# A new order of head pairs and projection tiles, merged products in latent attention, and two reordered steps at stage boundaries

## The reference: what is computed

```python
s_w = jnp.einsum('bqkgd,bskd->bkgqs', q_n, k_n).astype(jnp.float32) * scale      # windowed
p_w, p_c, _ = _multi_softmax([s_w, s_c, sink_col])
s_n = jnp.einsum('bwhd,bwnhd->bhwn', q_r, k_nb).astype(jnp.float32) * scale + bias.astype(jnp.float32)
```

```python
q = (_rmsnorm(c_q, q_norm) @ w_uq).reshape(B, S, MLA_HEADS, MLA_NOPE_DIM + MLA_ROPE_DIM)
q_rope = _apply_rope(q[..., MLA_NOPE_DIM:], cos[:, None], sin[:, None])
kv = (_rmsnorm(c_kv, kv_norm) @ w_ukv).reshape(B, S, MLA_HEADS, MLA_NOPE_DIM + MLA_V_DIM)
```

## Time and profile before

| | us |
|---|---|
| median of 3 runs | 2383.7 (2381.66 to 2384.02) |
| profiled execution, its own time | 2387.36 |
| its span, first to last instruction | 2386.1 |
| PE busy | 2279.2 (96%) |
| DVE busy | 1497.5 (63%) |
| ACT busy | 959.8 (40%) |
| mean granted TensorE clock | 0.979 |

### The profile page before, as it was taken

The page is one execution under the profiler, slowest core; times in us unless marked ns, Lnnn a source line. Parts: engine busy times, 40 slices in busy tenths (PEclk is TensorE's granted clock), DMA queues, the critical chain, the costliest instruction groups (busy, mean ns, idle before and its releaser), DMA issues. The chain is left out here.

```text
span 2386.1 us, 37057 instructions
## 1 busy us (share of the span) xinstructions
PE 2279.2 (96%) x14376; PEld 1925.4 (81%) x14376; DVE 1497.5 (63%) x2306; ACT 959.8 (40%) x1540; POOL 368.1 (15%) x365
## 2 busy tenths in 40 slices
PE   6999999998999999999999999879999999998998
PEld 4888887765678888878888876669998998798998
DVE  4666766545775666676664346466667766676874
ACT  4222223454542222242222245444446434555763
POOL 1000001000000000000000010039995476000000
PEclk9999999999999999999999999989999999999999
DMA  7554444111134444434443241114544332234544
GB/s 281 185 188 175 172 167 168 71 36 53 54 128 163 168 178 161 167 136 159 174 177 121 97 141 54 70 58 156 191 170 151 114 108 72 88 135 157 187 168 149
DMA packets 52615, 331.05 MB, mean 139 GB/s; under 512 B 6544, under 2 KB 7824, under 8 KB 21648
## 3 DMA queue, kind: packets, MB, share of 16 engines
q1 hardware_dynamic: 49040, 319.15, 37.0%
q0 software_dynamic: 3456, 10.25, 1.4%
HBM read 325.56 MB, written 3.80 MB: 138 GB/s over the span
## 5 line engine op out<-in xcount | busy, mean ns | idle before, releaser
L1181 PE MATMUL bank<-u_hi,whi 128*128 128x512 f32 (+1 forms) x2512 | 865.2, 344 | 29.2 <-DVE u_lo L1135 13.6
L1182 PE MATMUL bank<-u_lo,whi 128*128 128x512 f32 (+1 forms) x2512 | 849.8, 338 | 0.0
L1183 PE MATMUL bank<-u_hi,wlo 128*128 128x512 f32 (+1 forms) x2512 | 849.2, 338 | 0.0
L568 DVE TENSOR_TENSOR wlo<-raw,whi 128x2048 fp32r<-128x2048 f32 (+2 forms) x207 | 434.9, 2101 | 314.9 <-ACT whi L566 314.8
L1181 PEld LDWEIGHTS bank<-u_hi,whi 128*128 128x128 f32 x2512 | 477.3, 190 | 104.7 <-issue 30.3
L1183 PEld LDWEIGHTS bank<-u_hi,wlo 128*128 128x128 f32 x2512 | 477.4, 190 | 52.1
L1182 PEld LDWEIGHTS bank<-u_lo,whi 128*128 128x128 f32 x2512 | 477.5, 190 | 49.5 <-issue 0.2
L566 ACT ACTIVATE whi<-raw 128x2048 fp32r<-128x2048 f32 (+2 forms) x207 | 353.1, 1706 | 338.5 <-PE bank L1183 234.1
L1243 ACT ACTIVATE sil<-bank 128x512 f32<-128x512 f32 (+1 forms) x88 | 48.0, 545 | 543.6 <-PE bank L1183 543.5
L1181 PE MATMUL bank<-hidden_hi,whi 128*128 128x512 f32 x528 | 205.4, 389 | 0.0
L1182 PE MATMUL bank<-hidden_lo,whi 128*128 128x512 f32 x528 | 205.4, 389 | 0.0
(11 more groups left out here) (426 smaller groups left out, 2938.7 us busy)
## 6 DMA issues: line engine op xcount, KB each, us to landing
raw<-in_stream SPq DMA_DIRECT2D x231, 1024.0 KB, 4.8
raw<-in_stream SPq DMA_DIRECT2D x80, 704.0 KB, 4.0
first_ada<-in_stream SPq DMA_DIRECT2D x8, 1024.0 KB, 16.5
raw<-in_stream SPq DMA_DIRECT2D x8, 768.0 KB, 4.4
skew<-rpb_rows POOLq DMA_DIRECT2D x8, 336.0 KB, 6.1
nbr_bias<-skew POOLq DMA_DIRECT2D x24, 112.0 KB, 3.5
h<-in_tokens SPq DMA_DIRECT2D x1, 2048.0 KB, 11.6
uq_ukv<-in_small POOLq DMA_DIRECT2D x1, 1536.0 KB, 8.1
```

What stands on the lines that cost most here:

```text
L568: v.tensor_tensor(self.lo[to][:, 0:n], raw[:, 0:n], self.hi[to][:, 0:n].bitcast(F32), ALU.subtract).then_inc(self.s_lo, 1)
L1181: pe.q.matmul(dst, w[0], x[0], start=start, stop=False)
L1182: pe.q.matmul(dst, w[0], x[1], start=False, stop=False)
L1183: return pe.q.matmul(dst, w[1], x[0], start=False, stop=stop)
```

## The change

Four edits.

1. `ATT` becomes (3, 4, 0, 1, 5, 2, 6, 7) and `IN_TILES` follows it: q, k, v tiles of windowed pair 0 come right after those of the global pairs, the last tiles are q 7, k 4, v 4. The rotation products move with their tiles.
2. `nbr_masks` moves from before the first unit to the step behind tile 8 and the rotation of q 1. The generator is drawn before the first unit until the key of the global heads is ready.
3. `mla_inputs` makes q by two products of 128 columns of weights, and k of two heads at once by one product of 128 columns. The second key of a pair is copied by DVE from the upper partitions; a second copy of the signed sine is kept on partitions 96 to 127.
4. In `last_squares` with a second weighted square (the end of the first block) the quarter of whi comes behind the squares. In `w_o` the root table is loaded one group earlier.

```diff
-ATT = (3, 4, 5, 6, 7, 0, 1, 2)
-IN_TILES = [("q", 3), ("k", 1), ("q", 4), ("v", 1), ("q", 5), ("k", 2), ("v", 2), ("q", 6), ("k", 3), ("v", 3),
-            ("q", 7), ("k", 4), ("v", 4), ("q", 0), ("k", 0), ("v", 0), ("q", 1), ("q", 2)]
+ATT = (3, 4, 0, 1, 5, 2, 6, 7)
+IN_TILES = [("q", 3), ("k", 1), ("q", 4), ("v", 1), ("q", 0), ("k", 0), ("v", 0), ("q", 1), ("q", 5), ("k", 2),
+            ("v", 2), ("q", 2), ("q", 6), ("k", 3), ("v", 3), ("q", 7), ("k", 4), ("v", 4)]
...
-        if then:
+        if then and weighted is None:
             st.split_hi(PHASE[then], 1, 0)
...
         if weighted is not None:
             squared.append(weighted_done)
+            if then:
+                st.split_hi(PHASE[then], 1, 0)
...
-                    nbr_masks()
...
-                if i == 15:
+                if i == 6:
                     yield from turn("q", 0)
                     yield from turn("k", 0)
-            yield from v_turn(0)
-            yield from turn("q", 1)
-            yield from turn("q", 2)
+                elif i == 8:
+                    yield from turn("q", 1)
+                    nbr_masks()
+                    yield 0
+                elif i == 12:
+                    yield from turn("q", 2)
+            yield from v_turn(4)
...
-        while "nbr" not in prepared:
+        while ("k", 1) not in prepared:
             next(work)
...
+            trig_copied = dve.do(dve.q.tensor_scalar(swapped_sin, sin_t, cst("rope_sign", 1)[rp], None, ALU.mult))
...
             for i in range(2):
-                pe.q.matmul(bank[0:96, 0:S], uq[:, i, hh, 0:96], cq[:, i, :], start=(i == 0), stop=(i == 1))
-            for i in range(2):
-                pe.q.matmul(bank[rp, S:2 * S], uq[:, i, hh, 96:128], cq[:, i, :], start=(i == 0), stop=(i == 1))
-            zq = pe.do(pe.q.matmul(bank[0:64, S:2 * S], ukv[:, 0, hh * MN:(hh + 1) * MN], ckv[:, :], start=True, stop=True))
+                zq = pe.q.matmul(bank[:, 0:S], uq[:, i, hh, :], cq[:, i, :], start=(i == 0), stop=(i == 1))
+            if hh % 2 == 0:
+                zq = pe.q.matmul(bank[:, S:2 * S], ukv[:, 0, hh * MN:(hh + 2) * MN], ckv[:, :], start=True, stop=True)
+            zq = pe.do(zq)
...
-            a2 = act.do(act.q.activation(K2[0:64, hh, :], bank[0:64, S:2 * S], ACT.Copy))
+            if hh % 2 == 0:
+                copied = key_copied = act.do(act.q.activation(K2[0:64, hh, :], bank[0:64, S:2 * S], ACT.Copy))
             dve.after(zq, mla_ready.get(hh - 2))
+            if hh % 2 == 0:
+                next_key = dve.do(dve.q.tensor_copy(K2[0:64, hh + 1, :], bank[64:128, S:2 * S]))
...
-        if m.base == KC // 2 - 2:
+        if m.base == KC // 2 - 3:
             root_table()
```

More of the change, by code:

```diff
@@ L2080, in build @@
     cos_t, sin_t = [trig[rp, i, :] for i in range(2)]
+    swapped_sin = trig[96:128, 1, :]
     turns, ang = cos_t, sin_t
@@ L2376, in build @@
             dve.after(*trig_done)
+            trig_copied = dve.do(dve.q.tensor_scalar(swapped_sin, sin_t, cst("rope_sign", 1)[rp], None, ALU.mult))
+            dve.after(trig_copied)
             trig_ready = dve.do(dve.q.tensor_scalar(sin_t, sin_t, cst("rope_sign", 1)[rp], None, ALU.mult))
```

7 lines of the change are left out of this document (4 added, 3 removed).

## The result

| | before | changed |
|---|---|---|
| median of 6 runs, us | 2384.8 (2381.66 to 2389.97) | 2373.3 (2368.95 to 2374.33) |
| ratio of the times | | 0.9941, 95% interval 0.9925 to 0.9956 |
| profiled execution: its own time, its span, us | 2387.36, 2386.1 | 2373.76, 2372.4 |

A forecast was written before the change was run, and what follows sets the result against it. PE, busy 96% of the span, was taken to bound the kernel. Gains of 11 (second layer), 5 (first layer), 7 (latent attention), 1.4 and 0 (boundaries) sum to 24.4 us: 2383.7 - 24.4 = 2359.3 us, range 2353 to 2366.

The forecast's parts named there:

- What bounds the kernel: Whole kernel: PE, busy 96%; gains must cut its work or fill its waits, as for probabilities in the first block's attention.
- the open chain stays: Late attention units: own latency sets the pace, masks show in full; order and masks give 6 + 2, time 2367.3; chance 0.15.
- Edit 2, the masks: Both attention layers: masks and q 1's rotation block DVE for 5.0 us; between nothing and 5.0 shows, 1.5 taken per layer.
- Edit 1, second layer: Attention, 1500 to 1580: dense work between all units removes 10.5 of 12.75 us idle; the clock adds 2 (0 to 3.3).
- the filled stretch: Second layer's 40 us before 1500, dense work between units: PE idle 1.14 us, expected to hold through 1500 to 1580.
- slower: dense tiles wait for their banks: Both attention stages: tiles wait for ACT's copies to free banks; 15 waits of 2.26 us give 2393.2; chance 0.03.
- Edit 1, first layer: Attention, 560 to 600: 6.9 of 7.53 us idle goes; less 1.5 for the masks, taken as 5 (2 to 7).
- Edit 3: Latent attention: merged products remove 10.2 us of PE work, of which 7 (2 to 10.2) shows as DVE comes level.
- DVE sets latent attention's pace: Latent attention: DVE, with new key copies ahead of the rotations, leaves the merged products 1 us; time 2365.3; chance 0.15.
- Edit 4: Boundaries: squares at the first block's end start earlier, 1.4 us (1.0 to 1.5); earlier table load in w_o gains 0.
- the 24.4: Whole kernel: the forecast's total gain in us, 11 + 5 + 7 + 1.4 + 0.

The follow-up runs named there:

- e1: Changed kernel with the rotation of q 1 put into DVE's queue ahead of the masks; ratio to the kernel before 0.9924.
- e2: Changed kernel with the masks back at their old place, ahead of the first scores; ratio to the kernel before 0.9924.
- e9: e2 with copies of projection tiles out of their banks put ahead of the next pair's exps in ACT's queue; ratio to the kernel before 0.9891.

## Why the prediction was wrong

- **What bounds the kernel: right.** Transposes waited for probabilities because dense work had run out. With the new order those 6.7 us are gone and the clock is 1.00 in 1500 to 1580. The rival "the open chain stays" falls, though its time (2367.3) is nearer than the forecast's.
- **Edit 2, the masks: the step that failed in its reading.** The prediction had them right behind the small product for q 1, in the same place as its three rotation instructions, and took 1.5 us of a possible 5.0 in each layer. In truth the masks lie ahead of the rotation, and what is queued behind them is not a maximum with dense work to cover it but the scores of the next pair. Measured in the second layer: 3.70 us of idle PE and a clock of 0.57 in the four us behind, 4.2 to 4.4 us between the changed kernel and e1 (200.7 and 200.8 against 196.5 and 196.4). By the ratios 4.1 and, between the repeats, 5.0. In the first layer no such cost shows. That the whole bound of 5.0 was named, and 1.5 taken because DVE was half idle, was the mistake: the busy share says nothing of who needs the next instruction.
- **Edit 1, second layer: 10.5 + 2, failed in the sum.** Idle time "of the filled stretch, 1.14 us per 40" was carried over to all of the stage. The changed kernel has 4.96 + 2.39 + 5.14 = 12.5 us of idle PE in the 120 from 1460, where before had 13.9. Of that 3.7 is the masks. The rest is the mechanism of the rival "slower: dense tiles wait for their banks", given 0.03 with fifteen waits at 2.26 us. Its place was right and its number of waits was wrong: five bank waits in the second layer, 4.9 us, and four in the first, 6.6. In the kernel before they were 1.4 and 3.5 us. The argument against it, that tiles already stood so in the filled stretch, went by the idle share and not by the waits. In both kernels each such wait of a tile stands behind a `v_turn` or a `turn`, which has taken the second bank; the filled stretch has two, of only 0.61 and 0.52 us, and the new order has three of 1.7 us and more (1.74, 1.86, 2.17), where the old one had one (2.26). The price was also put on the wrong kind of time. Idle time from norm to norm fell by 0.2 us, and by 3.8 in e1, where the masks are out of the way (196.46 - 173.24 = 23.2), and not by 10.5. Busy time fell by 5.4 and 6.1, where the clock and latency had been given 2 with a bound of 3.3. So the 5.7 us gained here came mostly by a term that the sum held to be small.
- **Edit 1, first layer: 5, right in size, in part by luck.** 4.0 by the mean of four profiles with the new order and the moved masks (259.0, 262.9, 259.0, 260.9: 260.5) against the mean of three without (264.5). The masks' 1.5 did not show, and of the idle time in 520 to 640 us, 8.8 us before, 7.6 are left and not the forecast 2: the hole at 560 closed and one at 520 opened. Some 4 us more lay behind the bank waits (e2 to e9).
- **Edit 3: 7, right.** 6.5 by the profiles, 7.6 by the ratio of the edit alone. A product of 128 columns of weights costs no more than one of 96 did. The rival "DVE sets latent attention's pace" had the right engine for the missing 3.7 us, but let it take nearly all of the gain. That nothing would be won in the first step (6.35 us for 6.34) was forecast.
- **Edit 4: 1.4 and 0.** The squares start at once, as forecast, but this is worth 1.4 only when the panel is late; alone it made 0.7 with an interval from -1.4 to 3. The table made 0.2 by the rows, and nothing that the ratio shows.

In sum, by the runs: 7.4 for the order with the masks where they are, 7.6 for latent attention, the rest below notice: 15.0 against 14 measured. Of the 10 us that are missing from the 24.4, 4.1 are the masks. The rest is not told apart as well: what late copies cost the new order above the old one is 2.6 us by the ratios (7.9 - 5.3) and 6.1 by the profiles (4.1 + 4.8 - 2.8). With both mended the kernel is 26 us faster than before, at 2361, more than the forecast; some 5.3 of that the copies would have given in the old order too.

## What to carry to other kernels

When a diff moves instructions through a list of deferred work, read each engine's own queue at that place; the order in the source is not the order in the queue, and who needs the next instruction decides the cost, not how busy the engine is. When dense work is spread between the units of a pipeline, count what it shares with them, here two banks emptied by the engine that also does the exps, and put the copy that frees a bank ahead of long work that isn't urgent. An idle share measured in one stretch need not hold in the next: look at where its waits stand and what would make them longer. Split what a change gained into idle and busy time before saying which term was right. And repeat a profile before explaining 4 us of it: the same program twice differed by as much in one stage.

## What the runs showed of the hardware

A stage's time differs between executions of one program with the place of the half clock: in two profiles of the same instructions the first layer took 259.0 and 262.9 us, and the linear stage 143.0 and 139.4. The linear stage is 138.9 to 139.4 us in the seven profiles without a stretch of lower clock inside it and 141.3 to 144.7 in the seven with one. A wait of one length is not always followed by the lower clock: behind the same wait of 1.86 us the clock is 1.00 in the changed kernel (1504 to 1508) and falls in e2 (0.91 in 1498 to 1518). ScalarE's second key in place of VectorE's cost 1.3 us, though ScalarE is idle half the time: VectorE's rotation then waited for ScalarE's copies out of the same bank, 3.8 us in four waits.
